# Expert rows packed into 25 units of four 32-row strips, with experts ranked by the picks of six tiles, where 33 units of one expert each were

## What is computed

```
g_prob, g_idx = lax.top_k(p_group, 1)
...
e_prob, e_idx = lax.top_k(jax.nn.softmax(logit_e, axis=-1), TOP_K)
weight = g_prob * e_prob / jnp.sum(e_prob, axis=-1, keepdims=True)
...
hid = jax.nn.silu(xblk @ w_gate[e]) * (xblk @ w_up[e])
return hid @ w_down[e]
```

```
         all nine tiles                    the first six tiles
group 0  98  80  86  86  66  71  52  63    67 53 54 51 40 46 37 38
group 1  52  65  33  83  83  58  56  72    32 37 17 51 47 36 32 42
group 2  42  52  49  58  45  33  40  29    26 37 38 40 30 25 25 21
group 3  48 139  63 113  81 110 107  63    27 85 47 75 60 75 75 42
```

## Time and profile before

| | us |
|---|---|
| times of 3 runs | 1118.38, 1114.22, 3773.64 (median 1118.38) |
| the profiled execution | 1115.39 |
| its span, from the first to the last instruction | 1113.6 |
| PE busy | 1042.7 (94%) |
| DVE busy | 632.0 (57%) |
| POOL busy | 304.1 (27%) |
| ACT busy | 268.0 (24%) |
| mean granted TensorE clock | 0.971 |

### The profile page before, as it was taken

The page is one execution under the profiler, slowest core; times in us unless marked ns, Lnnn a source line. Parts: engine busy times, 40 slices in busy tenths (PEclk is TensorE's granted clock), DMA queues, the critical chain, the costliest instruction groups (busy, mean ns, idle before and its releaser), DMA issues.

```text
span 1113.6 us, 14260 instructions
## 1 busy us (share of the span) xinstructions
PE 1042.7 (94%) x4861; PEld 692.3 (62%) x4861; DVE 632.0 (57%) x1261; ACT 268.0 (24%) x593; POOL 304.1 (27%) x350
## 2 busy tenths in 40 slices
PE   3789999999978899999999999999999999999994
PEld 0334555555556556667776675877777777777772
DVE  1455555555566655675766778456755444445443
ACT  1232222222251232323323212221111111111110
POOL 1122222222231110110110000234445455444444
PEclk9799999999998899999999999799999999999998
DMA  9793333333254322332321129668989999988950
GB/s 306 283 404 125 145 144 145 145 145 126 80 168 130 88 109 97 142 115 67 142 84 59 77 97 389 235 228 345 345 300 351 343 361 345 348 339 341 355 188 18
DMA packets 78102, 229.80 MB, mean 206 GB/s; under 512 B 29835, under 2 KB 33566, under 8 KB 62294
## 3 DMA queue, kind: packets, MB, share of 16 engines
q1 hardware_dynamic: 50608, 198.86, 47.7%
q0 software_dynamic: 24048, 26.81, 7.2%
q10 hardware_dynamic: 3382, 3.32, 0.9%
HBM read 201.23 MB, written 88.25 MB: 260 GB/s over the span
## 4 chain that ended last, share of the span: by engine, by line
PE 81%; DVE 9%; DMA 2%; POOL 2%; issue 2%; ACT 1%; ACTq 1%; DVEq 0%; SPq 0%; POOLq 0%
PE bank L1045 13%; PE bank L1405 10%; PE bank L1407 10%; PE bank L1422 10%; PE bank L998 9%; PE bank L1215 9%; PE bank L1159 6%; PE bank L1185 5%; PE bank L1126 2%; PE bank L1010 2%; PE bank L1026 2%; DMA grope<-in_g_knorm 1%; POOL st L845 1%; PE bank L1056 1%; PE bank L1237 1%
## 5 line engine op out<-in xcount | busy, mean ns | idle before, releaser
L1045 PE MATMUL bank<-W_in,hT 128*128 128x512 f32 (+3 forms) x480 | 172.7, 542 | 3.7 <-DMA W_in<-in_w_in 3.7
L844 POOL TENSOR_SCALAR st<-st 128x1 f32<-128x1 f32 (+5 forms) x76 | 17.6, 231 | 549.6 <-DVEq L1779 251.4
L1045 PEld LDWEIGHTS bank<-W_in,hT 128*128 128x128 f32 (+1 forms) x480 | 80.1, 185 | 91.6 <-issue 84.4
L1422 PE MATMUL bank<-WD,hidT 128*128 128x512 f32 x264 | 118.9, 593 | 1.7 <-DVE hidT L2436 1.7
L1405 PE MATMUL bank<-WG,xT 128*128 128x256 f32 x528 | 119.5, 379 | 1.0 <-DVE xT L2420 1.0
L1407 PE MATMUL bank<-WU,xT 128*128 128x256 f32 x528 | 119.3, 379 | 0.0
L1215 PE MATMUL bank<-W_out,mT 128*128 128x512 f32 (+1 forms) x288 | 115.4, 563 | 0.1
L1407 PEld LDWEIGHTS bank<-WU,xT 128*128 128x128 f32 x528 | 100.3, 190 | 13.6
L1405 PEld LDWEIGHTS bank<-WG,xT 128*128 128x128 f32 x528 | 97.7, 190 | 13.1 <-issue 1.2
L2200 DVE COPY probT<-bank 128x512 f32<-128x512 f32 (+3 forms) x100 | 56.3, 563 | 57.3 <-PE bank L998 50.1
L1185 PEld LDWEIGHTS bank<-vall,probT 128*128 128x128 f32 x616 | 76.8, 192 | 15.6 <-issue 14.6
(11 more groups left out here) (333 smaller groups left out, 1438.0 us busy)
## 6 DMA issues: line engine op xcount, KB each, us to landing
WG<-in_w_gate_e SPq DMA_DIRECT2D x33, 1024.0 KB, 7.0
WU<-in_w_up_e SPq DMA_DIRECT2D x33, 1024.0 KB, 9.4
WD<-in_w_down_e SPq DMA_DIRECT2D x33, 1024.0 KB, 12.9
ada_w<-in_w_ada SPq DMA_DIRECT2D x24, 1024.0 KB, 7.9
residual_scratch<-x_att SPq DMA_DIRECT2D x32, 512.0 KB, 4.4
kbuf<-k_scratch SPq DMA_DIRECT2D x12, 384.0 KB, 5.1
xbuf<-in_x_prompt SPq DMA_DIRECT2D x8, 512.0 KB, 3.8
W_in<-in_w_in SPq DMA_DIRECT2D x2, 2048.0 KB, 22.3
```

The costliest lines, as they stand in the source:

```text
L1045: ins = mm(out, hT[:, place_of[t] % 2, k, :R], W_in[:, k, c0 + c.start:c0 + c.stop], start=(k == 0), stop=(k == KD - 1))
L1422: ins = mm(psum[5 + half][:], hidT[:, k, :], WD[u][:, k, half * 512:(half + 1) * 512], start=(k == 0), stop=(k == 1))
```

## The change

Ranks: inside each group the eight experts are ordered by their picks in the first six tiles (`sort_experts`, new, DVE). The expert of rank 0 gets room for 160 rows, ranks 1 and 2 128, ranks 3 and 4 96, ranks 5 to 7 64 (`CAPS`). The rooms are cut into strips of 32 rows, four strips to a unit, in the rank order `RANKS`; that makes 25 units. A unit now holds strips of one or two experts of one rank: 10 units hold one expert, 9 two experts with two strips each, 6 two experts with three strips and one. Units 18, 19, 23 and 24 hold two experts that no other unit uses; so do units 4 and 5.

```diff
+CAPS = (160, 128, 128, 96, 96, 64, 64, 64)
+RANKS = (1, 6, 0, 2, 4, 7, 3, 5)
+STRIP = 32
...
+MAXOV = 24
...
+def runs(unit):
+    starts = [i for i in range(SIDE) if i == 0 or unit[i] != unit[i - 1]]
+    width = SIDE if len(starts) == 1 else SIDE // 2 if starts == [0, SIDE // 2] else 1
+    return [(i * STRIP, width * STRIP, unit[i]) for i in range(0, SIDE, width)]
...
 def overflow_blocks(eng, n_ov, block):
-    with eng.If(n_ov > 1):
-        with eng.Fori(0, MAXOV - 1) as i:
-            with eng.If(i + 1 < n_ov):
-                block(i + 1)
+    with eng.If(n_ov > 0):
+        with eng.Fori(0, MAXOV) as i:
+            with eng.If(i < n_ov):
+                block(i)
             with eng.Else():
                 eng.nop()
...
+        for q in range(3, len(LOADS)):
+            e = expert(q)
+            if q >= SLOTS:
+                sp.wait_ge(s_gu, LAST_USE[LOADS[q - SLOTS]] + 1)
+            load_gate_up(e, q % SLOTS)
+            if q >= SLOTS:
+                sp.wait_ge(s_down, LAST_USE[LOADS[q - SLOTS]] + 1)
+            load_down(e, q % SLOTS)
...
+        def gu(m):
+            pe.wait_ge(s_xTa, m + 1)
+            pe.wait_ge(s_xTv, m + 1)
+            gate_up_loaded(UNITS[m], m)
+            out = psum[2 + m % 2][:].rearrange("p (a n) -> p a n", a=2)
             for k in range(KD):
-                mm(psum[2][:, 0:DE], xT[:, k, :], WG[u][:, k, :], start=(k == 0), stop=(k == KD - 1))
+                for c, n, x in runs(UNITS[m]):
+                    ins = mm(out[c:c + n], xT[:, k, c:c + n], WGU[LOADS.index(x) % SLOTS][:, :, k, :], start=(k == 0), stop=(k == KD - 1))
+            ins.then_inc(s_gu, 1)
```

More of the change, by code:

```diff
@@ L562, in uses @@
             return [("rb", 1)]
+        if work == "rankA":
+            return [("ranks", 1)]
         if work == "x2T":
@@ L2468, in _ @@
         dve.wait_ge(s_sums, 2)
[L2469 removed]
+        decode(slice(0, NU), psum[7][:, NU:2 * NU], psum[7][:, 2 * NU:3 * NU])
         signal(s_tab)
[L2471 removed]
+        for b in range(NU):
             hidT_(b)
[L2473 to L2479 removed]
+            gate(b, b % 2)
+            if b + 1 < NU:
+                hidden(b + 1)
+            if b + 2 < NU:
+                xT_half(b + 2)
+            add_rows(b, b % 2, b % NG, 16 * (b // NG + 1))
             if b == 0:
```

507 lines of the change are left out of this document (254 added, 253 removed).

## The result

The changed kernel takes 1193.28 us (median of 4 runs, 1193.03 to 1193.93) against 1116.3 us for the kernel before: a ratio of 1.070, 95% interval 1.0667 to 1.0732. One of the four runs of the kernel before took 3773.64 us, and the ratio leaves it out. It is slower, as forecast, but by 7% and not by 3%; 1193 lies above the range's upper end of 1180. The profiled execution took 1193.07 us, its span is 1191.3, and all that follows is about these 39 us above the forecast span of 1152 (39.7 above the sum of its terms, 1151.6).

What follows compares the result with a forecast made beforehand. TensorE, busy for 94% of the span, was taken as the bound. From 1113.6 us, -80.1 for seven periods, +2 strips, +47 waits and clock and +69 after down(24) gave span 1152, execution 1153; range 1115 to 1180.

Steps and rivals of the forecast that it cites:

- the waits: Units 19, 20 and 24 wait 10.3 us each for new experts' weights, unit 23 6 us: +37 us, bounds 28 and 46.
- the clock: TensorE's clock falls after each of the four waits, costing 2.5 us each: +10 us, bounds 0 and 26.
- the serial end: After down(24) come two serial blocks, last sum and scatters, empty passes and the finish: 89.6 us, where 20.6 followed down(31).
- landings of scatters in the blocks: In each block at the end, the three scatters before it land in 1.5 us, with register work another 1.5.
- strips: In 15 of 25 units, products on 64 or 32 columns run side by side; layout changes cost 0.1 us a unit, +2.
- Fewer units: Packed expert stage: 33 units become 25 at 11.44 us each; down(24) ends at 1012.9 if nothing waits.
- Sorting and the closing: Last attention tile and closing: moved picks and removed waits offset the added DVE work; net 0, bounds -3 and +4.
- ten small operations in `code` and `place`: Added DVE work on the path to the token numbers, some 0.2 us each, 1.5 us for the wide ones.
- The blocks: Two serial blocks at the end, 32 us each, the second waiting for the first's scatters: 64 us, bounds 50 and 80.
- The end: After the blocks: 8 us for last sum and scatters, 10 for 22 empty POOL passes (bounds 4 and 25), 7.6 to finish.
- the end costs more: Rival, 13%: branch code fetches, landings as under load and 1 us passes make the blocks 80 and passes 25: 1184 us.
- The pairs don't wait: Rival, 20%: at units beginning two experts, places free early enough or loads flow faster; 47 us go: 1106, no change.

Runs made afterwards that it cites:

- room that fits: The changed kernel with room for 160, 128, 128, 128, 96, 96, 64, 64 rows by rank, 27 units and no block at the end: 1096.1 us, ratio 0.985.
- the fastest kernel: The changed kernel with fitting room, held-back down loads, spread ranks, sorting on GpSimd, and VectorE's wait and placing moved to the closing: 1069.5 us, ratio 0.958.

## Why the prediction was right and wrong

The direction was right, and so were the waits, the clock and the serial end as mechanisms. One step failed, the work added on DVE, and several terms were too small, nearly all of them on the same side. The two largest of these are the waits (+13.8) and the landings of scatters in the blocks. Added up, the bounds that the terms were given reach from about 1109 to 1213 us; the range of 1115 to 1180 left out most of the upper part, as if the errors would cancel.

| term, up to down(24) | forecast | measured |
|---|---|---|
| last attention tile and closing | 0 | +11.3 |
| strips | +2 | about +9 |
| waits for weights | +37 | +50.8 |
| clock behind the waits | +10 | +13.1 |
| last unit, without a successor | 0 | -5.4 |
| rest | 0 | -0.7 |
| sum | 49 | 78.1 |

*Fewer units.* Right. A unit of one expert has a period of 11.39 us (two of them, 889.13 to 900.52), 0.05 less than before. The starting point was a little off: down(31) of the kernel before has gate and up of unit 32 (8.1 us with transposes) ahead of it, which the last packed unit has not; against that its down product waits 2.70 us for the hidden rows. That is the -5.4.

*Strips.* Right that they run side by side, wrong by a few us on the price. A product of four strips takes 7.07 us and of two 7.09, against 7.03. A period with a gate and up product on strips and a full-width down product is longer by 0.3 us (912.01 to 923.70, 11.69), one with both on strips by 0.6 (923.70 to 935.67, 11.97), so a unit on strips costs some 0.6 us, with two experts' halves as with a strip and three. Fifteen such units make about 9, against +2, for which no row had been shown. By the Trainium skill (TensorE: Matmul & The Clock Gate, What overlaps and what doesn't) weight loads that share their row group aren't hidden, by the prediction's estimate 2.6 us in each unit of 32-column strips; the trace shows 0.6, so that doesn't bind here.

*The waits.* The mechanism and the four places were right: reordering the queue alone took away 33 of 50.8 us. The size of each was not. From the first issue to use the three loads of unit 19 take 13.3 us instead of 2.4 + 7.7 + 0.5 = 10.6, because I let them pass through an otherwise idle DMA with 0.5 us for gathers; 1.5 MB of other traffic goes through beside them. And units 5 and 18, which I had let fit "just", waited 2.3 and 1.4 us, and unit 7, which begins one expert and which the forecast didn't name, 2.6; behind units 5 and 7 stand products at the low clock. Here a fit without slack became a wait.

*The clock.* The mechanism was right: at the end of the wait of unit 19 the granted clock is 0.50, the 1.2 GHz level:

```profile
973.00:975.00 2.00, 0.84 (x2) 0.32 (x4) 0.00 (x0) 0.00 (x0) 0.00 (x0) 0.50 1.03 424
```

The four products behind the waits of 7.7 to 13.2 us took 1.3 to 2.7 us more than 7.09, 7.9 us in all where the forecast had 10. Units 5 and 7 and the first gate product (8.94 us), which it had not counted, add 5.3.

*Sorting and the closing.* This is the step that failed. "3.5 us of sorting in head 5, beside a TensorE that has other work there" took TensorE's work for cover. It isn't, since that work ends in a product which needs DVE's copy, and in the traces that copy starts only after the picks or the sorting issued ahead of it. DVE was busy for 5.7 and 7.1 of 8 us there before, so what was added to a head came out as delay of its copy. The picks' new place has the same flaw, and the "ten small operations in `code` and `place`" lay in a closing in which TensorE waits for DVE. What the runs showed in place of "net 0" is +11.3: 4.0 for the picks, 4.9 for the sorting and 4.2 for the operations in the closing, less 1.9 for the wait that goes. The bounds of -3 and +4 were far too narrow for three pieces of serial DVE work of 4 to 5 us each.

*The blocks.* 75.3 us against 64. Landing was the mis-sized term: the scatters took 7.0 and 5.4 us, with the weights beside them, where 1.5 was taken and part of 1.5 for register work. Without the weights a pair of blocks took 65.5. The prediction called the weights' transfer "hidden behind these" and asked only whether it was in time, not whom it delays. The rest is mostly one down product that ran at the low clock (6.77 us where 3.6 was taken).

*The end.* The 22 passes cost 12.7 us (forecast 10, bounds 4 and 25) and what follows the last scatter is shorter by as much. By the Trainium skill (Advanced Engine Details and Errata, Control Flow Timing) a pass would be an estimated 0.32 us; the run shows 0.58.

Of the rivals, "the end costs more" was right in part, by the landings under load; its passes of 1 us were not, and no run tested whether code had to be fetched. That its 1184 us lies nearest to the measured time is luck, since the larger part of the miss lies ahead of the blocks. "The pairs don't wait" fell.

## What to carry to other kernels

When work moves onto an engine beside a busy TensorE, ask which copy in that engine's queue TensorE needs next and what now stands ahead of it; free time summed over a stretch is no cover. When a schedule frees two buffers at once, look at the order in the load queue first: a load that waits for the later release holds up those that could have gone. And a general block at the serial end, 38 us here, costs more than three packed units (11.4 us each), so on this input room that fits beat room that is tight.

## What the hardware showed that I had not expected

A scatter or gather of at most 128 rows that meets a 3 MB load landed 3 to 5 us later (scatters 7.0 us against 2.1 and 5.4 against 2.4, gathers 7.0 against 1.7 and 7.5 against 2.2), and moving the load merely chose which of the two is delayed. Products on strips of 32 columns, with the weight loads of all four, took 7.07 us against 7.03 for one of full width. An empty pass of the loop cost 0.58 us at the end of the span. GpSimd took 15.4 us for the sorting and the tables that take DVE some 7, and the fastest kernel has it there, with nobody waiting for it early; whether it needs to be there, no run shows.
